# Projections back to the residual with tokens as stationary side and 512 weight columns moving; residual, sums of squares and output by tokens

## The reference

```python
# block 1
h  = x + (g_ssm * (mamba2(...) @ w_out_ssm) + g_lru * (rglru(...) @ w_out_lru)) @ w_out
hn = rmsnorm(h, norm2_w)
gate, up = split(hn @ w_ffn_in)                       # 2 x 2816 columns
h  = h + (silu(gate) * up) @ w_ffn_out
x  = rmsnorm(h, norm_f_w)
# block 2, two layers
for layer in range(2):
    h = rms_norm(x, attn_norm_w[layer]); proj = h @ w_in_2[layer]
    x = x + concat(retention, sparse attention, dilated attention) @ w_out_2[layer]
    h = rms_norm(x, mlp_norm_w[layer])
    x = x + square(relu(h @ w_up[layer])) @ w_down[layer]   # 4096 wide
return rms_norm(x, final_norm_w)
```

## Time and profile before

| | |
|---|---|
| time | 1312.67 us, median of 3 runs (1312.04 to 1313.08) |
| the profiled execution | 1314.49 us, its span 1313.2 us |
| busy share of the span | PE 94%, PEld 91%, DVE 65%, ACT 50%, POOL 35% |
| matmuls | 9852, mean granted clock 0.977 |
| chain that ended last | PE 78%, DVE 13%, ACT 6% |
| weights moved | 209 MB at a mean of 159 GB/s |

### The profile page before, as it was taken

One profiled execution on the slowest core, in us unless ns is written; L12 is line 12 of the kernel. 1 busy time (PEld: TensorE's weight loads), 2 busy tenths in 40 slices (PEclk: granted clock), 3 DMA queues, 4 the chain that ended last, 5 costly groups with the idle time before them and its releaser, 6 DMA issues.

```text
span 1313.2 us, 23221 instructions
## 1 busy us (share of the span) xinstructions
PE 1235.0 (94%) x9852; PEld 1196.2 (91%) x9852; DVE 847.4 (65%) x1070; ACT 657.1 (50%) x857; POOL 464.3 (35%) x160
## 2 busy tenths in 40 slices
PE   4989799999999999999989999999999898999996
PEld 3889699999999999999988799999999788999996
DVE  5789987987555655557677375455466864755553
ACT  4767476676435433435435853333344286533332
POOL 1324334557844111111445423222224552322221
PEclk9999899999999999999889999999989899999998
DMA  8435455554555655655433245555554333455540
GB/s 243 148 98 161 157 188 173 190 161 154 185 176 178 221 174 180 193 176 153 130 97 130 96 161 193 185 174 188 162 159 128 116 120 128 162 192 171 183 161 32
DMA packets 153974, 209.37 MB, mean 159 GB/s; under 512 B 7536, under 2 KB 134672, under 8 KB 153232
## 3 DMA queue, kind: packets, MB, share of 16 engines
q1 hardware_dynamic: 150080, 201.34, 47.2%
q10 hardware_dynamic: 3792, 6.55, 1.5%
HBM read 206.80 MB, written 1.08 MB: 158 GB/s over the span
## 4 chain that ended last, share of the span: by engine, by line
PE 78%; DVE 13%; ACT 6%; issue 2%; DMA 1%; POOL 0%; ACTq 0%; SPq 0%; DVEq 0%; POOLq 0%
PE bank L491 77%; DVE w_lo L1199 2%; ACT w_hi L856 2%; DVE xbc L1207 1%; ACT tmp L856 1%; ACT act_hi L856 1%; ACT L856 1%; PE bank L499 1%; DVE residual L1199 1%; DVE work L1203 1%; DVE act_lo L1207 1%; DVE tmp L1199 1%; DVE score L1199 1%; DVE rk_t L1199 1%; DVE tmp L1207 1%
## 5 line engine op out<-in xcount | busy, mean ns | idle before, releaser
L491 PE MATMUL bank<-act_hi,w_hi 128*128 128x256 f32 x2920 | 847.7, 290 | 36.5 <-DVE w_lo L1199 17.0
L491 PE MATMUL bank<-act_lo,w_hi 128*128 128x256 f32 x2920 | 835.2, 286 | 0.0
L491 PE MATMUL bank<-act_hi,w_lo 128*128 128x256 f32 x2920 | 834.6, 286 | 0.0
L491 PEld LDWEIGHTS bank<-act_hi,w_hi 128*128 128x128 f32 x2920 | 569.3, 195 | 48.9 <-issue 38.2
L491 PEld LDWEIGHTS bank<-act_lo,w_hi 128*128 128x128 f32 x2920 | 569.2, 195 | 1.1 <-issue 0.5
L491 PEld LDWEIGHTS bank<-act_hi,w_lo 128*128 128x128 f32 x2920 | 568.8, 195 | 0.0
L1199 DVE TENSOR_TENSOR w_lo<-raw,w_hi 128x2048 fp32r<-128x2048 f32 (+4 forms) x179 | 379.0, 2119 | 261.4 <-ACT w_hi L856 261.3
L856 ACT ACTIVATE w_hi<-raw 128x2048 fp32r<-128x2048 f32 (+1 forms) x191 | 360.4, 1890 | 373.1 <-PE bank L491 371.7
L1705 POOL TENSOR_TENSOR w_lo<-raw,w_hi 128x1280 fp32r<-128x1280 f32 (+6 forms) x94 | 318.2, 3387 | 415.2 <-ACT w_hi L856 406.6
L1705 POOL TENSOR_TENSOR act_lo<-tmp,act_hi 128x512 fp32r<-128x512 f32 x52 | 133.3, 2569 | 407.0 <-ACT act_hi L856 407.0
L1199 DVE TENSOR_TENSOR tmp<-bank,rstd 128x512 f32<-128x512 f32 x43 | 29.7, 691 | 52.6 <-PE bank L491 52.5
(11 more groups left out here) (203 smaller groups left out, 851.5 us busy)
## 6 DMA issues: line engine op xcount, KB each, us to landing
raw<-in_w_in SPq DMA_DIRECT2D x64, 1024.0 KB, 5.2
raw<-in_w_up SPq DMA_DIRECT2D x32, 1024.0 KB, 5.4
raw<-in_w_down SPq DMA_DIRECT2D x32, 1024.0 KB, 4.8
raw<-in_w_ffn_in SPq DMA_DIRECT2D x22, 1024.0 KB, 5.1
raw<-in_w_out SPq DMA_DIRECT2D x12, 1024.0 KB, 4.8
raw<-in_w_ffn_out SPq DMA_DIRECT2D x11, 1024.0 KB, 4.9
raw<-in_w_out_ssm SPq DMA_DIRECT2D x8, 1024.0 KB, 4.9
raw<-in_w_out_lru SPq DMA_DIRECT2D x5, 1024.0 KB, 4.8
```

The lines of the kernel that those rows point to most:

```text
L491: return mm_ops.matmul(out, lhs, rhs, start=start, stop=stop, skip_group_check=True)
```

## The change

`residual` becomes 128 tokens x 2 token tiles x 1024 channels. In `out`, `ffn_out`, `out_2` and `down` the tokens of `act_hi` and `act_lo` are now stationary (128 of them) and 512 weight columns move; the four banks are two token tiles by two halves of the channels (`place`). Since a norm's input must have channels on partitions, PE transposes `residual` into PSUM (`turn`): half of it before the last quarter of the last row tile, half in `opening`, which interleaves the first two column tiles after a norm. ACT and DVE make `act_hi` and `act_lo` from PSUM. Squares are summed along the free axis by ACT's accumulator into columns of `cols`; root and reciprocal are of 128 x 2. `row` spreads the reciprocal along tokens with two small float32 products by the identity. In the MLPs the reciprocal is no longer applied to `up` but, squared, as `gain` in the addition to the residual; ACT takes the Relu. The weights of the two final norms come by DMA as rows, in two buffers of the attention; x comes a second time, by tokens. `final` stores by tokens, its first token tile before the last two quarters are added.

```diff
-    put("after", ("ffn_gate", 0), ("scale", 0), ("evac", "ffn_gate", 0))
+    put("after", ("ffn_up", 0), ("scale", 0), ("row", 0), ("evac", "ffn_gate", 0))
+    put("mid", ("ffn_gate", 1), ("evac", "ffn_up", 0))
...
-        put("after", ("up", NF2 * l + 1), ("scale", n + 1), ("evac", "up", NF2 * l), ("evac", "up", NF2 * l + 1))
+        put("after", ("up", NF2 * l + 3), ("scale", n + 1))
...
+        def place(n, b):
+
+            t, h = (b // 2, b % 2) if n == 5 else (b % 2, b // 2)
+            return t, slice(h * 512, (h + 1) * 512), 2 * h + t
...
+                if i == T["bc", 0]:
+                    nc.sync.dma_start(res[:, :, :], x_tok.rearrange("(t p) c -> p t c", p=P)).then_inc(sem("x_tok_arrived"), 16)
...
+                    nc.sync.dma_start(row_f, rows_w[0:1, :].partition_broadcast(P)).then_inc(sem("row_f_arrived"), 16)
+                if i == T["up", NF2 + 8]:
+                    sp.wait_ge(*at("dil1_s", 8))
+                    nc.sync.dma_start(row_out, rows_w[1:2, :].partition_broadcast(P)).then_inc(sem("row_out_arrived"), 16)
...
+            def turn(n, half):
+
+                pe.wait_ge(*at("res_added", 4 * n + 2 * half + 2))
+                for k in range(4 * half, 4 * half + 4):
+                    if k % 2 == 0:
+                        bank = take(low if n in (2, 4) else high, ("turned", n, k // 2), at("xn_lo", DC * n + k + 2))
+                    for t in range(TT):
+                        c0 = (k % 2) * SEQ + t * P
+                        inst = transpose(bank[:, c0:c0 + P], res[:, t, k * P:(k + 1) * P])
+                    if k % 2:
+                        inst.then_inc(*tick("turned"))
+
+            def opening(i, n):
+
+                tiles = []
+                for i2 in (i, i + 1):
+                    name, j = TILES[i2]
+                    bank = take(high if name == "up" else low, (name, j), freed_by(name, j))
+                    tiles.append((i2, bank, range(shapes[i2][1] // P)))
+
+                def part(tile, half):
+                    i2, bank, chunks = tile
+                    hi, lo = tile_ready(i2)
+                    for m in chunks:
+                        for k in range(4 * half, 4 * half + 4):
+                            norm_ready(n, k)
+                            inst = product(bank[:, m * SEQ:(m + 1) * SEQ], hi[:, k, m * P:(m + 1) * P],
+                                           lo[:, k, m * P:(m + 1) * P], act_hi[:, 8 + k, :], act_lo[:, 8 + k, :],
+                                           m == 0 and k == 0, k == DC - 1)
+                    if half:
+                        inst.then_inc(*tick("tile_used"))
+
+                part(tiles[0], 0)
+                turn(n, 1)
+                part(tiles[1], 0)
+                part(tiles[0], 1)
+                stages("after", i)
+                part(tiles[1], 1)
+                stages("after", i + 1)
...
+            def token_rows(i, name, j, whole, first, last, ring, hi, lo, k0):
+
+                n = {"out": 0, "ffn_out": 1, "out_2": 2 + 2 * whole, "down": 3 + 2 * whole}[name]
+                for b in range(4):
+                    if name == "out_2" and b == 2:
+                        stages("mid", i)
+                    if last and b == 3 and n < 5:
+                        turn(n, 0)
+                    if first:
+                        acc[name, b] = take(ring, (name, whole, b), freed_acc(name, whole, b))
+                    bank = acc[name, b]
+                    t, columns_of, _ = place(n, b)
+                    for j2 in range(2):
+                        inst = product(bank, act_hi[:, k0 + j2, t * P:(t + 1) * P], act_lo[:, k0 + j2, t * P:(t + 1) * P],
+                                       hi[:, j2, columns_of], lo[:, j2, columns_of], first and j2 == 0, last and j2 == 1)
+                    if last and b < 3:
+                        inst.then_inc(*tick("acc_done"))
+                inst.then_inc(*tick("tile_used"))
...
+            def row(n):
+
+                bank = take(high, ("row", n), at("row", {0: 1, 1: 2, 3: 3}[n]))
+                pe.wait_ge(*at("xn_rstd", {0: 1, 1: 3, 3: 5}[n]))
+                pe.wait_ge(sem("consts_arrived"), 16)
                 for t in range(TT):
-                    inst = transpose(bank[:, t * P:(t + 1) * P], rstd[:, t * P:(t + 1) * P])
-                inst.then_inc(*tick("rstd_turned"))
+                    inst = mm(bank[:, t * P:(t + 1) * P], by_col[:, t:t + 1].broadcast_to([P, P]), c["ident"])
+                inst.then_inc(*tick("row_mm"))
...
+                if name == "up":
+                    act.wait_ge(*used(name, j))
+                    act.wait_ge(*at("h_hi", NF1 + j - 2))
+                    act.wait_ge(*at("h_lo", NF1 + j - 2))
+                    fn(tmp[j % 3][:, :], bank, ACT.Relu).then_inc(*tick("up_relu"))
...
+                for k in range(DC):
+                    act.wait_ge(*at("turned", DC // 2 * n + k // 2 + 1))
+                    fn(act_hi[:, 8 + k, :], psum["turned", n, k // 2][:, (k % 2) * SEQ:(k % 2 + 1) * SEQ], ACT.Copy,
+                       scale=weight(k)).then_inc(*tick("xn_hi"))
                 for b in range(4):
-                    act.wait_ge(*at("res_added", 4 * n + b + 1))
-                    for k in {0: (), 1: (0, 1), 2: (2, 3, 4, 5), 3: (6, 7)}[b]:
-                        fn(act_hi[:, 8 + k, :], res[:, k, :], ACT.Copy, scale=weight(k)).then_inc(*tick("xn_hi"))
-                act.wait_ge(*at("xn_mean", n))
-                for b in range(4):
-                    fn(pair(tmp[6 + b][:, :]), res[:, 2 * b:2 * b + 2, :], ACT.Square).then_inc(*tick("xn_sq"))
+                    t, columns_of, col = place(n, b)
+                    fn(tmp[6 + b][:, :], res[:, t, columns_of], ACT.Square, accum=sq[:, col:col + 1]).then_inc(*tick("xn_sq"))
+                if n == 1:
+                    act.wait_ge(*now("xn_sq"))
+                    for b in range(4):
+                        t, columns_of, col = place(n, b)
+                        act.wait_ge(*at("xw", b + 1))
+                        fn(tmp[6 + b][:, :], x_w[t][:, columns_of], ACT.Square, accum=sq_w[:, col:col + 1]).then_inc(*tick("xw_sq"))
...
+                act.wait_ge(*at("xn_total", n + 1 + (n > 1)))
+                fn(root, total, ACT.Sqrt, scale=1 / D, bias=eps[:, :]).then_inc(*tick("xn_root"))
...
             def add_residual(n, b):
                 name, _ = LAST_OUT[n]
                 whole = (0, 0, 0, 0, 1, 1)[n]
+                t, columns_of, _ = place(n, b)
+                r = res[:, t, columns_of]
                 vec.wait_ge(*(at("acc_done", 6 + 3 * n + b + 1) if b < 3 else used(*LAST_OUT[n])))
-                r = res[:, 2 * b:2 * b + 2, :]
-                tt(r, r, pair(psum[name, whole, b]), ALU.add).then_inc(*tick("res_added"))
+                vec.wait_ge(sem("x_tok_arrived"), 16)
+                if n in (1, 3, 5):
+                    stt(r, psum[name, whole, b], gain[:, t:t + 1], r, ALU.mult, ALU.add).then_inc(*tick("res_added"))
+                else:
...
+                def low_part(k):
+                    vec.wait_ge(*at("xn_hi", DC * n + k // 2 * 2 + 2))
+                    if n == 1:
+                        vec.wait_ge(*now("w_norms"))
+                    stt(act_lo[:, 8 + k, :], psum["turned", n, k // 2][:, (k % 2) * SEQ:(k % 2 + 1) * SEQ], weight(k),
+                        act_hi[:, 8 + k, :].bitcast(F32), ALU.mult, ALU.subtract).then_inc(*tick("xn_lo"))
...
                 if n == 2:
-                    vec.wait_ge(*at("f_sq", 4))
-                for b in range(4):
+                    vec.wait_ge(*now("res_normed"))
+                for b in range(3):
                     add_residual(n, b)
-                    for k in {0: (), 1: (0, 1), 2: (2, 3, 4, 5), 3: (6, 7)}[b]:
-                        vec.wait_ge(*at("xn_hi", DC * n + k + 1))
-                        vec.wait_ge(*now("w_norms") if n == 1 else now("res_added"))
-                        stt(act_lo[:, 8 + k, :], res[:, k, :], weight(k), act_hi[:, 8 + k, :].bitcast(F32), ALU.mult,
-                            ALU.subtract).then_inc(*tick("xn_lo"))
-                add_up(6, 4, "xn_sq", 4 * n, "xn_total")
+                low_part(0)
+                low_part(1)
+                add_residual(n, 3)
+                for k in range(2, DC):
+                    low_part(k)
+                if n == 1:
+                    vec.wait_ge(sem("row_f_arrived"), 16)
+                    vec.wait_ge(*now("res_added"))
+                    for b in range(4):
+                        t, columns_of, _ = place(n, b)
+                        tt(x_w[t][:, columns_of], res[:, t, columns_of], row_f[:, columns_of], ALU.mult).then_inc(*tick("xw"))
...
+                done = {0: 1, 1: 2, 2: 4, 3: 5, 4: 6}[n]
+                vec.wait_ge(*at("xn_sq", 4 * n + 4))
+                add_squares(total, sq)
+                vec.wait_ge(*at("xn_root", done))
+                if n != 1:
+                    ops.reciprocal(by_col, root).then_inc(*tick("xn_rstd"))
```

(52 more changed lines are left out.)

194 lines of the change are left out of this document (93 added, 101 removed).

## The result

The changed kernel takes 1306.38 us (median of 5 runs, 1305.4 to 1307.54) against 1312.67 for the kernel before (5 runs, 1311.53 to 1314.54): ratio 0.9949, 95% interval 0.9939 to 0.996. It is faster by 0.5%, where I had predicted 1290 and a range that ended at 1304. The profiled spans are 1305.2 and 1313.2 us, 8.0 apart.

What follows compares the result with a forecast made beforehand. PE alone was taken to set the pace in steady work, but not at the five boundaries between a projection and the next norm. -31.7 + 1.8 + 12.5 - 4.9 = -22.3, against the median 1312.67: 1290 us, range 1280 to 1304.

Steps and rivals of the forecast that it cites:

- the edits that I cost at nothing: In steady work: up evacuation by ACT, one DVE product less in ffn_gate, new row DMAs; cost put at 0.
- Term 1: Row tiles: 2640 matmuls of 0.120 us become 1320 of 512 columns at 0.216 us, saving 31.7 us.
- rival B: Row tiles: 13.3 ns come with every matmul, 0.2267 us each, 17.6 us saved, total 1304; chance 0.09.
- the bound (0.240): Row tiles: cost of a 512-column matmul goes by columns, 0.240 us each, nothing saved.
- The give-back in attention: `out_2` tiles among attention steps: PE waits for DVE and ACT there, so 1.8 us of the saving is lost.
- Term 2: Five boundaries from a projection to the next norm: new waits and transposes, 35.6 against 23.0 us, 12.5 us lost.
- Term 3: The end: from last addition to span end 8.3 us instead of 13.2, a gain of 4.9 us.
- C: Every row tile: main type streams at 9/8 of the clock's time, 0.240 us a matmul, total 1320; chance 0.05.
- D: Boundaries: waits and transposes bring seven more half-clock stretches, 12 us, total 1302; chance 0.08.
- E: Row tiles: 512 columns cost what 256 do, 158 us saved, total about 1160; chance 0.01.

Runs made afterwards that it cites:

- experiment 1: A separate program of matmul blocks alone on TensorE, varying columns, type, bank and stationary tile; 512-column fp32r matmuls came 0.2266 us apart.
- experiments 5 and 6: Changed kernel with ScalarE's split of the next weight tile ahead of the squares, 1299.68 us; or with norm 0's scale one weight tile earlier, 1302.51 us.
- the four moves: Changed kernel with low parts 2 and 3 before the fourth addition, split before squares, norm 0's scale one tile earlier, first addition before split: 1287.81 us.
- experiments 4 and 7: Changed kernel with low parts 2 and 3 before the fourth residual addition, 1306.09 us; or VectorE's first addition before its split part, 1306.31 us.

## Why the prediction was wrong, point by point

**What bounds the kernel.** Right: column tiles are unchanged to 0.01 us each, no wait of PE is ended by a DMA, `up` with its new evacuation takes 5.76 us as before; the edits that I cost at nothing cost nothing.

**Term 1: the step that failed.** I reasoned that the 13.3 ns "appear only where streaming is as short as the weight load" and took 0.216 from the float32 rows as "the nearest". It is 0.2267, rival B: experiment 1 has the 13.3 ns at 384 and 512 columns as at 256, and 2.5 ns for float32. The float32 rows were near in length but of another type; the only rows of the right type, carried 13.3, and the half-clock row, where the extra vanishes, does not speak against a fixed cost: the 512-column matmuls of the changed kernel have none there either (0.427 us), and 13.3 ns at full clock. The term is 17.6 at full length (1320 x 0.0133) and not 31.7; the trace shows 16.5. I had the bound (0.240) and the rival; giving the rival a chance of 0.09 was the mistake, since the only rows of that type spoke for it.

**The give-back in attention.** 1.8 predicted, 1.0 found, for the reason given: three `out_2` tiles a layer save 0.39 us together instead of 0.90.

**Term 2.** 12.5 predicted, 14.1 found. Each wait came at its place and nearly in its size: transposes 0.44 (0.8 predicted), low part 0.55 (0.85), `row` 3.11 (3.0), `ki` 3.56 (4.35), behind just the instructions named. Missing were the clock's shares at n = 0 and n = 1 (a stretch of 3.4 us and one of 6.8 more); too dear were n = 2, 3 and 4, by 1 us each.

**Term 3.** 4.9 predicted, 5.9 found. The queue of VectorE was as described, but the first token tile's root and product were done sooner: addition 2 began 0.1 after PE's end and not 0.7, the last product ended at 4.4 and not 5.5, and the span at 7.4 and not 8.3.

**Rivals.** B was the case; its 1304 was 2.4 too low. C (0.240, slower) falls at 0.2267. D held in less than a third of its size: 6.8 us more at half clock than before (58.0 against 51.2 before the end), not 24; but experiments 5 and 6 show that a removed wait can pay through the clock too. The transposes alone do not bring the clock down: with the four moves the 16 of n = 0 stand in the stretch from 402 to 436, at clock 1.00. E falls at 0.2267. With 0.2267 in Term 1, the 1.0 given back, and all else as predicted the sum is -17.6 + 1.0 + 12.5 - 4.9 = -9.0, against -8.0 between the traces and -6.3 between the medians.

## What to carry to other kernels

The extra beyond the columns' streaming time belongs to a matmul type: measure it on rows of the same type, or in a program of nothing but such matmuls, before a change of shape is priced by it. With fp32r and 128 stationary columns, halving the number of matmuls by 512 moving columns is worth 13.3 ns for each one saved, not a share of the time. And a layout change that adds short steps to four queues is to be laid out again step by step: here it put 14 us (waits, transposes and half clock) at five places, and four moves of single steps took some 20 out (18.6 by the medians), three times what the change itself had given.

## What the runs showed that I had not expected

- fp32r matmuls with 128 stationary columns cost 13.3 ns beyond their columns at 256, 320, 384 and 512 columns (15.8 at 448), and no block of them comes faster than 111 ns a matmul in the mean (58 with 64 stationary columns); bf16 costs 2.5 ns, as a float32 record does, and goes down to 56 ns at 128 columns and 25 at 8. A pair of the two in turn costs 17.5 ns more than the sum. At clock 0.50 the 13.3 ns are not seen: 512 columns come every 427 ns.
- VectorE and GpSimd, each reading two SBUF inputs, are served in turn: 1.22 becomes 3.36, or 2.35 becomes 3.5, by which of two starts 0.08 us apart is served first. Together with where the first half-clock stretch falls this moves a trace by about 1.4 us with no change of program there.
- The time at half clock outside the end lay between 41 and 65 us in ten traces of nearly the same program. A gain of 2 to 4 us, shown by the tile starts, can vanish in it (experiments 4 and 7).
